# Tables in parts, xh on ScalarE, records in two parts, turns inside products: a two-block fp32 kernel

## The reference

```python
# first block: retention and pooling, then a conv FFN, each closed by a layer norm
q, k, v, g, p = split(x @ w_in)                 # 512 columns each
q, k = rope(q), rope(k) * 128 ** -0.5
ret = rmsnorm_per_head(retention(q, k, v)) * silu(g)
mix = concat(ret, pool_mixer(p) * pool_scale) @ w_out
x = layernorm(ALPHA * x + mix)
x = layernorm(ALPHA * x + (silu(conv3(x @ w_gate)) * (x @ w_val)) @ w_down)    # 2816 wide
# second block
u = rms_norm(x, mix_norm[0]) @ ssm_w_in         # 64 groups of 16 channels
y = S5 scan of u (64 complex states a group) + d * u;  z = gelu(y)
x = x + (z @ w_glu)[:, :1024] * sigmoid((z @ w_glu)[:, 1024:])
x = x + swiglu_ffn(rms_norm(x, ffn_norm[0]))    # "f2"
h = rms_norm(x);  ckv = h @ w_kv_a;  cq = h @ w_q_a      # latents of 288 and 384
x = x + attention(16 heads from rms_norm(cq) @ w_q_b and rms_norm(ckv) @ w_kv_b) @ w_o
x = x + swiglu_ffn(rms_norm(x, ffn_norm[1]))    # "f3"
```

## Time and profile before

| | |
|---|---|
| time, median of 3 runs | 1910.47 us (1909.74 to 1915.1) |
| profiled execution | 1913.36 us, span 1911.6 us |
| mean granted clock of TensorE | 0.971 of full |
| busy: PE, DVE, ACT, POOL | 1812.7, 818.8, 652.8, 698.2 us |
| chain that ended last | PE 79%, DVE 14%, ACT 3%, DMA 3% |

### The profile page before, as it was taken

The page is one execution under the profiler, slowest core; times in us unless marked ns, Lnnn a source line. Parts: engine busy times, 40 slices in busy tenths (PEclk is TensorE's granted clock), DMA queues, the critical chain, the costliest instruction groups (busy, mean ns, idle before and its releaser), DMA issues.

```text
span 1911.6 us, 22662 instructions
## 1 busy us (share of the span) xinstructions
PE 1812.7 (95%) x9038; PEld 1516.4 (79%) x9038; DVE 818.8 (43%) x1430; ACT 652.8 (34%) x1102; POOL 698.2 (37%) x315
## 2 busy tenths in 40 slices
PE   6889999899999699999999999998999999999999
PEld 5777878688788478878988888877878898888887
DVE  3686779769856714502311011134766331011111
ACT  3133235226254322222422222245655342222221
POOL 4222334325444230033344444433460244534342
PEclk9999999899999798999999999998999999999999
DMA  9322234354545345622332323322200133332332
GB/s 224 67 78 67 78 108 144 115 161 133 176 121 184 116 176 187 227 68 76 111 98 90 99 88 101 93 69 74 82 23 1 56 99 94 94 99 88 100 94 83
DMA packets 236793, 202.73 MB, mean 106 GB/s; under 512 B 39952, under 2 KB 197776, under 8 KB 234640
## 3 DMA queue, kind: packets, MB, share of 16 engines
q1 hardware_dynamic: 231968, 173.64, 30.4%
q10 hardware_dynamic: 4720, 27.64, 4.0%
HBM read 175.55 MB, written 25.69 MB: 105 GB/s over the span
## 4 chain that ended last, share of the span: by engine, by line
PE 79%; DVE 14%; ACT 3%; DMA 3%; issue 1%; POOL 0%; DVEq 0%; SPq 0%; ACTq 0%
PE ps L356 12%; PE ps L358 12%; PE ps L357 12%; PE ps L380 9%; PE ps L382 9%; PE ps L381 9%; PE ps L411 2%; PE ps L413 2%; PE ps L412 2%; DMA rec<-s_records 2%; PE ps L776 2%; PE ps L795 2%; PE ps L687 1%; PE ps L786 1%; PE ps L436 1%
## 5 line engine op out<-in xcount | busy, mean ns | idle before, releaser
L907 POOL TENSOR_TENSOR w_lo<-w_raw,w_hi 128x1024 fp32r<-128x1024 f32 (+4 forms) x284 | 670.4, 2371 | 1175.8 <-ACT w_hi L1023 1175.3
L356 PE MATMUL ps<-a_hi,w_hi 128*128 128x512 f32 (+1 forms) x1184 | 443.6, 375 | 10.8 <-DVE q_t L1655 6.3
L358 PE MATMUL ps<-a_hi,w_lo 128*128 128x512 f32 (+1 forms) x1184 | 441.6, 373 | 0.0
L357 PE MATMUL ps<-a_lo,w_hi 128*128 128x512 f32 (+1 forms) x1184 | 441.6, 373 | 0.0
L1023 ACT ACTIVATE w_hi<-w_raw 128x1024 fp32r<-128x1024 f32 (+4 forms) x284 | 284.6, 1015 | 271.7 <-DMA w_raw<-in_ffn_w_gate_up_dram 71.9
L356 PEld LDWEIGHTS ps<-a_hi,w_hi 128*128 128x128 f32 x1184 | 223.9, 189 | 51.8 <-issue 6.7
L358 PEld LDWEIGHTS ps<-a_hi,w_lo 128*128 128x128 f32 x1184 | 223.8, 189 | 39.2
L357 PEld LDWEIGHTS ps<-a_lo,w_hi 128*128 128x128 f32 x1184 | 223.8, 189 | 38.6
L1896 DVE TENSOR_TENSOR ev<-ps,xh 128x512 f32<-128x512 f32 x44 | 30.4, 692 | 417.6 <-PE ps L358 397.6
L380 PE MATMUL ps<-w_hi,h_hi 128*128 128x512 f32 x476 | 190.6, 400 | 11.1 <-DVE h_lo L1390 8.6
L382 PE MATMUL ps<-w_hi,h_lo 128*128 128x512 f32 x476 | 189.4, 398 | 0.0
(11 more groups left out here) (338 smaller groups left out, 2412.3 us busy)
## 6 DMA issues: line engine op xcount, KB each, us to landing
w_raw<-in_ffn_w_gate_up_dram SPq DMA_DIRECT2D x88, 512.0 KB, 3.8
rec<-s_records ACTq DMA_DIRECT2D x16, 1440.0 KB, 6.2
w_raw<-in_w_up_dram SPq DMA_DIRECT2D x44, 512.0 KB, 4.0
w_raw<-in_ffn_w_down_dram SPq DMA_DIRECT2D x40, 512.0 KB, 3.6
s_records<-stage SPq DMA_DIRECT2D x16, 928.0 KB, 6.1
w_raw<-in_w_in_dram SPq DMA_DIRECT2D x20, 512.0 KB, 4.1
w_raw<-in_w_down_dram SPq DMA_DIRECT2D x20, 512.0 KB, 4.4
w_raw<-in_ssm_w_glu_dram SPq DMA_DIRECT2D x16, 512.0 KB, 3.6
```

Source lines behind the costliest of these rows:

```text
L356: pe.matmul(bank, wh, xh_, start=first, stop=False)
L357: pe.matmul(bank, wh, xl_, start=False, stop=False)
L358: return pe.matmul(bank, wl, xh_, start=False, stop=last)
L907: pool.tensor_tensor(w_lo[:, n % RING, 0:w], w_raw[:, n % RING, 0:w], w_hi[:, n % RING, 0:w].bitcast(F), ALU.subtract).then_inc(lo_made, 1)
```

## The change

- x is turned in the middle of a chunk (`inside`), one chunk earlier than before.
- The product k takes banks that no reader of q holds (`pass_banks`), and the S5 parameters are turned inside k's product; ACT copies them out.
- `s5_tables` is cut in four: the tables ahead of the rope of k, `s5_turns` behind it, `s5_powers` ahead of the cuts of `ret_t`, `s5_inputs` behind them. The input matrices are made in four steps instead of two.
- In f1 the last `h_lo` of a group is made ahead of `s5_phases` instead of behind it (`finish_split`).
- `xh` of mix0 is made by ACT; its gain goes into ssm_w_in's chunks. ACT makes the first two chunks of u ahead of the last `s5_batch_out`.
- A record comes in as a state part (two transfers of 768 and 512 columns) and an out part (1600 columns), each with its own semaphore, issued by SP as soon as the part's last reader is through.
- kv_a has three chunks instead of four, `ckv_t` is turned inside q_a, `cq_t` behind the first latent product, the latent order is (0,0), (0,1), (1,0), and the rope tables are made in f2.

```diff
...
-LATENT_ORDER = [(0, 0), (1, 0)] + [(0, c) for c in range(1, 4)] + [(1, c) for c in range(1, 4)]
-N_CONST, N_TURNED, N_PARAM = 12, 8, 5
+LATENT_ORDER = [(0, 0), (0, 1), (1, 0), (0, 2), (0, 3)] + [(1, c) for c in range(1, 4)]
+N_CONST, N_TURNED, N_PARAM = 13, 8, 5
...
+                        if inside and t == TT // 2:
+                            inside(n)
...
+            def turn_parameters(n):
+
+                if n == 1:
+                    pe.wait_ge(turn_in, 16 * N_TURNED)
+                    pass_banks(XC)
...
-            for i, nm in enumerate("qkvg"):
-                if nm == "v":
-                    turn_parameters()
-                rows_product(nm, w_in0, a_hi, a_lo, KT, i * HALF, HALF, XC, wait_k=(lambda k: k + 1) if i == 0 else None,
-                             between=(lambda n: turn_input(XC * n)) if i == 0 else None)
+            rows_product("q", w_in0, a_hi, a_lo, KT, 0, HALF, XC, wait_k=lambda k: k + 1,
+                         inside=lambda n: turn_input(XC * (n + 1)))
+            pass_banks(XC + TT)
+            rows_product("k", w_in0, a_hi, a_lo, KT, HALF, HALF, XC, between=turn_parameters)
...
+                rows_product(("u", half), ssm_w_in_2[0], a_hi, a_lo, KT, half * HALF, HALF, 2, gain=2,
+                             wait_k=(lambda k: mixed - (k < KT // 2)) if half == 0 else None)
...
-            rows_product("q_a", mla_w_q_a_2[0], a_hi, a_lo, KT, 0, QR, 2, gain=1)
-
-            turn_rows("ckv_t", lambda t, k: ckv[:, t, k * P:k * P + P], KVR // P,
-                      ready=lambda t: pe.wait_ge(ckv_ready, t + 1), through_ev=True)
-            kv_split = n_split[0] - TT
-            cq_split = n_split[0]
-            turn_rows("cq_t", lambda t, k: cq[:, t, k * P:k * P + P], QR // P,
-                      ready=lambda t: pe.wait_ge(cq_ready, t + 1), through_ev=True)
+            def turn_keys(n):
+
+                if n == 2:
+                    turn_rows("ckv_t", lambda t, k: ckv[:, t, k * P:k * P + P], KVR // P,
+                              ready=lambda t: pe.wait_ge(ckv_ready, t + 1), through_ev=True)
+
+            kv_split = n_split[0]
+            cq_split = kv_split + TT
+            rows_product("q_a", mla_w_q_a_2[0], a_hi, a_lo, KT, 0, QR, 2, gain=1, between=turn_keys)
...
+        def load_state_part(eng, b_):
+
+            for o, w in ((W_O, P_O - W_O), (C_O, REC - C_O)):
+                eng.dma_start(rec[b_ % 3][:, o:o + w], rec_dram[b_, :, o:o + w]).then_inc(rec_state[b_ % 3], 16)
+
+        def load_out_part(eng, b_):
+
+            eng.dma_start(rec[b_ % 3][:, P_O:C_O], rec_dram[b_, :, P_O:C_O]).then_inc(rec_out[b_ % 3], 16)
...
+                if n == chunks_at[("u", 1, TT - 1)] + RING:
+                    for b_ in range(NB - 3):
+                        sp.wait_ge(zc_ready, b_ + 1)
+                        load_state_part(sp, b_ + 3)
+                        sp.wait_ge(*closed(("y", b_)))
+                        load_out_part(sp, b_ + 3)
...
+                                if down_batch[g, half] == NB:
+                                    limit[0] = chunks_at[("u", 0, 0)] - 1
+                                    make(limit[0])
...
+            ln_deviation(down, 1, 0)
             for t in range(TT):
-                ln_deviation(down, 1, t)
-                if t:
+                deviation("mix0", down, whole, t)
+                if t + 1 < TT:
+                    ln_deviation(down, 1, t + 1)
+                act.wait_ge(rms_made, t + 1)
+                act.activation(xh[:, t % 2, :], x_rows[:, t, :], ACT.Copy, scale=st[:, 8 + t:9 + t])\
+                   .then_inc(xh_ready, 1)
...
+                if nm == "k":
+                    s5_tables()
...
-            s5_tables()
+            s5_turns()
...
+            s5_powers()
             for g in range(RH):
                 split(("ret_t", g), *row_split(a_hi, a_lo, g))
+            s5_inputs()
...
+                    if f in up_phases or f == f1 - 1:
+                        finish_split()
                     if f in up_phases:
                         s5_phases(up_phases[f])
...
+            def rms(t):
+                v.wait_ge(sq_ready, t + 1)
+                v.reciprocal(st[:, 8 + t:9 + t], st[:, 4 + t:5 + t]).then_inc(rms_made, 1)
...
+                        if stage == "f2" and f == 2:
+                            rope_angles()
+                        if stage == "f2" and f == 6:
+                            rope_tables()
...
-            first_group = {(1, 2): first_keys, (2, 2): first_queries, (2, 3): first_rope, (3, 0): first_scaled}
+            first_group = {(1, 2): first_keys, (2, 1): key_rope, (3, 2): first_queries, (3, 3): first_rope, (4, 0): first_scaled}
```

More of the change, by code:

```diff
@@ L115, in program @@
         ident = fixed("ident", [P, P], F)
-        gains = fixed("gains", [P, 2, KT], F)
+        gains = fixed("gains", [P, 3, KT], F)
         kva_g = fixed("kva_g", [P, 2], F)
@@ L360, in rows_product @@
             def rows_product(stage, w, ah, al, nk, c0, cn, per, row0=0, wait_k=None, wait_t=None, between=None,
-                             gain=None, first_k=0):
+                             gain=None, first_k=0, inside=None):
                 stage = stage if isinstance(stage, tuple) else (stage,)
@@ L1001, in step @@
                 act.wait_ge(act_step, steps[0])
-            made = [0]
+            made, limit = [0], [10 ** 6]
             def ahead(count):
@@ L1125, in ffn @@
                         split_ev((stage, "val", f), *row_split(h_hi, h_lo, f - f0))
+                        if stage == "f2" and f == 4:
+                            rope_trig()
                         if swish_from_conv and up_batch.get(f):
@@ L1141, in _ @@
                 act.activation(a_hi[:, k, :], full(act, ("x", k)), ACT.Copy).then_inc(hi_ready, 1)
-            ahead(chunks_at["lam"])
-            act.wait_ge(*closed(("c", 1, 1)))
+            release("lam", act.activation(lam[:, 0:2, :].rearrange("p a g -> p (a g)"), at("lam")[:, 0:P], ACT.Copy))
+            for i in range(2):
+                for h in range(2):
+                    o = c_p[:, i, 32 * h:32 * h + 32, :].rearrange("p g k -> p (g k)")
+                    b = at(("c", i, h))
+                    step(act.activation(o[0:NS], b[0:NS], ACT.Copy))
+                    release(("c", i, h), act.activation(o[NS:P], b[NS:P], ACT.Copy, scale=-1.0))
             act.wait_ge(p_in, 16 * N_PARAM)
@@ L1201, in _ @@
             whole = lambda t: (ln_ready, t + 1)
+            ln_deviation(down, 1, 0)
             for t in range(TT):
-                ln_deviation(down, 1, t)
-                if t:
+                deviation("mix0", down, whole, t)
[4 more added lines that the diff above has]
+                   .then_inc(xh_ready, 1)
+                if t and t < TT - 1:
                     split_tile("mix0", t - 1, to_a_s5)
-                deviation("mix0", down, whole, t)
+            split_tile("mix0", TT - 2, to_a_s5)
             split_tile("mix0", TT - 1, to_a_s5)
+            limit[0] = 10 ** 6
+            make(chunks_at[("u", 0, 0)] + 1)
             for i in range(2):
@@ L1534, in s5_tables @@
                 v.wait_ge(p_in, 16 * N_PARAM)
[L1535 to L1543 removed]
+                v.wait_ge(*freed[bank_no["lam"]])
+                v.wait_ge(*freed[bank_no["c", 1, 1]])
                 for i in range(2):
@@ L1578, in s5_tables, with s5_powers @@
                 go(v.tensor_scalar(turn[:, 1, :, :], turn[:, 2, :, :], -1.0, None, ALU.mult))
+                settle()
+            def s5_powers():
+                s = lambda i: sm[:, i, :]
+                sn, cs, r = s(7), s(8), s(3)
+                lr, li = lam[:, 0, :], lam[:, 1, :]
+                go(v.memset(pri[:, 0, 0, :], 1.0))
+                go(v.memset(pri[:, 1, 0, :], 0.0))
+                go(v.tensor_tensor(pri[:, 0, 1, :], r, cs, ALU.mult))
+                go(v.tensor_tensor(pri[:, 1, 1, :], r, sn, ALU.mult))
+                settle()
                 for lo_, n in ((1, 1), (1, 2), (1, 4)):
@@ L1889, in _, with rope_angles, rope_tables @@
                 add_glu(0, t)
+            def rope_angles():
+                v.wait_ge(m_in, 16 * 7)
+                go(v.memset(gcol[NOPE:QK, :], 1.0))
+                step(v.tensor_copy(st[:, 130:134], pos_i[:, :]))
+                for t in range(TT):
+                    go(v.tensor_scalar(rot[:, 0, 4 + t, :], frq[:, :], st[:, 130 + t:131 + t], None, ALU.mult))
+                settle()
+                reduced(rot[:, 0, 4:8, :], rot[:, 1, 4:8, :], rot[:, 0, 0:4, :])
+                quarter(rot[:, 1, 0:4, :], rot[:, 0, 0:4, :]).then_inc(tab_dve, 1)
+            def rope_tables():
+                v.wait_ge(tab_act, 6)
+                for i, (fn, half) in enumerate(((0, 0), (1, 1), (1, 0), (0, 1))):
+                    g = hg[:, ROPE + half * ROPE // 2:ROPE + (half + 1) * ROPE // 2].unsqueeze(1)\
+                        .to_broadcast([P, TT, ROPE // 2])
```

(5 more changed lines are left out.)

169 lines of the change are left out of this document (77 added, 92 removed).

## The result

The changed kernel takes 1868.07 us (median of 4 runs, 1867.6 to 1869.83). Its ratio to the kernel before on the same chip is 0.9771, 95% interval 0.9754 to 0.9788: 2.3% faster. The forecast was 1867. The profiled execution took 1867.94 us, with a span of 1866.1 and a mean granted clock of 0.983 (0.971 before).

The account below looks back on a forecast made before the run. PE, busy 95% of the span, was taken as the bound. Terms 12.2 - 2 + 7.5 + 11 + 14.5 = 43.2 us took the profiled 1913.4 to 1870.2; with medians 2.9 lower, 1867 was predicted, range 1860 to 1875 (chance 0.45).

Parts of the forecast that it names:

- Start: Up to f1's layer norm: 26.3 us from removed waits, minus 14.1 for w_out's second half delayed by DVE; net +12.2.
- three prices of the clock: At the start, estimated PE time lost at low clock: 3.0 and 2.2 us behind two gaps, 1.7 per later gap.
- f1: First feed of `h_lo`: its 8.6 us wait goes, but PE stands as long for adds; -2, bounds -3 and +11.5.
- mix0: Norm chain for `xh`: DVE freed of multiplications and POOL, some 10.7 us, less 3.3 for later `k_s`; net +7.5.
- S5 loop: Record waits of 6.0 us and three low clocks go through earlier state parts issued by SP; +11, bounds 0 and +12.
- Latent stage: mla: kv_a in three chunks and ckv turned inside q_a remove waits and lost clock; +14.5, bounds 9 and 16.
- Rival E: S5 records: three transfers queue in a row, up to 15 us a record, making the kernel slower; 1947 at 10.7; chance 0.02.
- nine waits of the earlier trace: PE's waits before the change: the largest nine said to come to 64 us, seven of them for DVE.

Follow-up runs that it names:

- cuts_first: The changed kernel with the cuts of `ret_t` ahead of the powers, powers and inputs both between cuts and adds: 1873.65 us, ratio 0.9803.
- phases_late: The changed kernel with the second `s5_phases` behind the first adds of f1's first group: 1853.8 us, ratio 0.9696.
- u_in_norm: The changed kernel without the two chunks of u made ahead of the last batch; ACT makes them inside the second norm: 1873.96 us, ratio 0.978.
- parts_on_act: The changed kernel with both parts of each S5 record issued by ACT behind the gelu instead of by SP: 1868.74 us, ratio 0.9755.
- kv_four: The changed kernel with kv_a in four chunks of two column tiles instead of three of three: 1870.78 us, ratio 0.977.
- rope_back: The changed kernel with the second rope's angles, sines and tables back in the latent stage instead of f2: 1874.62 us, ratio 0.9798.
- one_record: The changed kernel with each S5 record loaded whole again, issued by SP: 1876.94 us, ratio 0.9798.

## Why the prediction was right

The steps, in its own order.

- **Start: right in place, mechanism and size.** The waits for `rtmp`, `lam` and `q_t` went, and the retention's last multiplication stands 27.0 us earlier (155.33 for 182.29; 26.3 forecast). The cut was forecast at 200.8 in the old clock of events less 26.3, that is 174.5; PE went on at 173.79. POOL caught four instructions, two in each pair. The second half was forecast 12.4 later than without the powers: 204.9 - 26.3 + 12.4 = 191.0, measured 190.27. cuts_first shows that the adds set this start. The three prices of the clock (3.0, 2.2 and 1.7 us) had no row behind them but the mean clock; the matmul starts give 2.9, 2.1 and, behind the two new waits, 1.5 and 1.7.
- **f1: right mechanism, the term was mis-sized,** -2 for -2.9. The wait is 11.39 instead of 8.60 us, with the same low clock behind it, 2.9 and 2.8. I had "the same 8 us a product later". But the second add ended 6.0 us behind the cut of `h_lo` in DVE's old list, and what PE had left of the first half takes only 4.9 at the full clock; and DVE came to the adds 9.9 us earlier than before (353.39 for 363.24), PE to its product 11.2 earlier. The list from the end of the diagonal to the adds is not what grew: it lasts 25.7 us before (from 337.57) and 26.0 now (from 327.40), and POOL catches four instructions in each (2.15, 2.44, 2.79 and 3.26 us before, 2.80, 3.42, 3.32 and 2.89 now). The delay came in ahead of it, where the cut at 320.41 was caught (2.25 us, before 0.68 at 332.09). That the meeting with POOL makes this part is read from the traces and was not tested. Two clock effects of 1.3 us, which I did not foresee, cancel: a longer low clock behind the wait for `w_lo` at f1's start, and none any more behind the third group's wait. The low bound was -3. phases_late shows that without the phases ahead of the adds there is no wait.
- **mix0: right mechanism, mis-sized, +7.5 for +9.2.** The loss was 2.4 us instead of 3.3: PE closed the last record's product at 618.3, and ACT copied `k_s` at 620.71, behind the chunk:

```profile
616.95 1.33 ACT L1055 ACTIVATE w_raw<-w_raw,gains 128x512 f32<-128x512 f32 x2 [0.92 <-DMA w_raw<-in_ssm_w_in_dram]
...
620.71 0.59 ACT L1130 ACTIVATE k_s<-ps 16x512 f32<-16x512 f32 x1
```

  The gain from there to u was 11.5 us (7.3 to 18.85) instead of 10.7. DVE's norm instructions were all free of POOL; the four caught before (2.55, 3.31, 2.59 and 3.25 us) come to the 6.6 of the estimate. That this freeing was what the early chunks were worth, I had only argued, and u_in_norm says otherwise for the changed kernel: with them late, ACT's own list costs 4.7 and 3.4 us and POOL 1.75.
- **S5 loop: right size, wrong reason in part.** The waits and their clock went (+12.3 for +11). The prediction gave this to the earlier issue and to SP; parts_on_act has neither and is as fast. What counts is that line 703 waits for 640 KB instead of 1440.
- **Latent stage: right size (+14.9 for +14.5), not settled in its parts.** The waits for `ev` (3.6 us) and for q_a's chunk went, but the turning inside q_a, to which the sum gave 6.6 of the 14.5, was not undone in any run. The 3.8 us for q_a's chunk went, but not by kv_a's three chunks alone, as I had it: kv_four and rope_back each leave it at 0.5 us or less. That either is enough would explain both; a kernel with both undone was not run. The rope tables, which the sum had at nothing, with 5 us if their cover were gone, cost 5 to 6.5 us in rope_back (1874.62 against 1868.07, ratios 0.9798 and 0.9771 with intervals that overlap), of which the trace shows a wait of 4.09.
- **Rival E, three transfers in a row on a queue,** has its answer in the DMA view: 4.4 and 4.9 us (and 5.0 for the third, of 256 KB), three of them in a batch of 5.6 us (sixteen from 699 to 789), without a wait. They overlap, at 217 GB/s over the loop. The rule of the Trainium skill on batching to 1 MiB (DMA: Bandwidth & Descriptors, section "Measured"), taken at its figure for 64 KB, as the rival did, would have made the change slower; here transfers of 256 to 800 KB that overlap lose nothing that PE sees, and the whole record of 1440 KB is the slower choice (one_record).
- The other rule of the Trainium skill, on DVE and POOL (SBUF, section "Who interferes with whom"), agrees with the four catches ahead of the cuts: 2.36 to 2.43 us for a product that lasts 0.23.

One reading ahead of the sum was wrong and carries nothing: the nine waits of the earlier trace rows come to 64 us, but they are not the nine largest. With 6.9 us for the first tiles of x and 4.5 for `w_lo`, both left out there, the nine largest come to 68 us, and six of them are waits for DVE.

That the total lies within 1.1 us of the forecast is in part luck. The terms miss by +0.3, -0.9, +1.7, +1.3, -0.6 and +0.4, together 2.2: the profiled execution was forecast at 1870.2 and took 1867.94. The median came closer only because of the 2.9 us taken off for the distance between median and profiled execution, and in the changed kernel this distance is 0.1.

## What to carry to other kernels

Before moving work into an idle stretch of DVE, look at what POOL does in that stretch: here each POOL instruction of 2.4 us made one two-operand DVE instruction at least as long as itself (2.36 to 2.43 us for 0.23), so 8.1 us of small ones needed 17. Where a wait of PE for DVE is removed by reordering, look for the next thing in the same list that PE needs (here the adds); in f1 moving the work behind that one too gave the time back (14 us). And a load of which one part is needed earlier was worth a semaphore for each part here, whoever issued it.
